# Softmax-attention scores as three products of rounded parts and rests

## The reference, cut to what matters

```
q = apply_rope(q, cos, sin) * (DA_DH ** -0.5)
k = apply_rope(k, cos, sin)
s = jnp.einsum('bhmqd,bhmkd->bhmqk', q_blk, k).astype(jnp.float32)
p = jax.nn.softmax(s, axis=-1)
a = p[:, :, 0] - lam * p[:, :, 1]
```

## Time and profile before

| what | value |
|---|---|
| median of 3 runs | 2431.71 us (2431.59 to 2432.74) |
| the profiled execution | 2431.39 us, span 2429.6 us |
| TensorE matmuls busy | 2413.4 us, 99% of the span |
| VectorE busy | 1827.1 us, 75% |
| ScalarE busy | 1300.5 us, 54% |
| GpSimd busy | 201.6 us, 8% |
| TensorE's share of the chain that ended last | 95% |

### The profile page before, as it was taken

The page is one execution under the profiler, slowest core; times in us unless marked ns, Lnnn a source line. Parts: engine busy times, 40 slices in busy tenths (PEclk is TensorE's granted clock), DMA queues, the critical chain, the costliest instruction groups (busy, mean ns, idle before and its releaser), DMA issues.

```text
span 2429.6 us, 40806 instructions
## 1 busy us (share of the span) xinstructions
PE 2413.4 (99%) x16410; PEld 2250.9 (93%) x16410; DVE 1827.1 (75%) x2403; ACT 1300.5 (54%) x2014; POOL 201.6 (8%) x236
## 2 busy tenths in 40 slices
PE   9999999999999999999999999999999999999998
PEld 9999989898999999888899998999989999998887
DVE  6666777754888998978585567777648889999784
ACT  6444666543555556556454456664436555554563
POOL 0001022100200000003100011111002000000031
PEclk9999999999999999999999999999999999999999
DMA  5454444254323233833233544343543232346421
GB/s 178 139 177 139 137 133 146 102 180 152 105 72 96 87 103 106 302 113 130 97 128 125 180 146 140 127 134 107 192 148 105 72 90 83 107 159 250 149 100 61
DMA packets 290411, 321.52 MB, mean 132 GB/s; under 512 B 10416, under 2 KB 223920, under 8 KB 290224
## 3 DMA queue, kind: packets, MB, share of 16 engines
q1 hardware_dynamic: 215744, 171.39, 22.6%
q10 hardware_dynamic: 74480, 147.53, 16.7%
HBM read 253.60 MB, written 65.27 MB: 131 GB/s over the span
## 4 chain that ended last, share of the span: by engine, by line
PE 95%; ACT 2%; issue 1%; DVE 1%; DMA 1%; POOL 0%; ACTq 0%; SPq 0%; DVEq 0%; POOLq 0%
PE ps L862 23%; PE ps L1142 14%; PE ps L1324 13%; PE ps L1087 9%; PE ps L835 5%; PE ps L1430 5%; PE ps L1070 5%; PE ps L1293 3%; PE ps L1260 3%; PE ps L849 3%; PE ps L1040 2%; PE ps L914 1%; PE ps L1410 1%; PE ps L1059 1%; PE ps L971 1%
## 5 line engine op out<-in xcount | busy, mean ns | idle before, releaser
L2048 DVE TENSOR_TENSOR wlo<-raw,whi 128x1024 fp32r<-128x1024 f32 (+1 forms) x152 | 163.8, 1079 | 55.1 <-ACT whi L3016 55.1
L862 PE MATMUL ps<-hT_hi,whi 128*128 128x384 f32 x608 | 203.1, 334 | 0.0
L862 PE MATMUL ps<-hT_hi,wlo 128*128 128x384 f32 x608 | 203.1, 334 | 0.0
L862 PE MATMUL ps<-hT_lo,whi 128*128 128x384 f32 x608 | 203.1, 334 | 0.0
L3030 ACT ACTIVATE U<-ps 128x384 f32<-128x384 f32 x152 | 74.8, 492 | 223.8 <-PE ps L862 223.8
L1324 PE MATMUL ps<-whi,PH_hi 128*128 128x512 f32 x456 | 179.1, 393 | 0.0
L1324 PE MATMUL ps<-whi,PH_lo 128*128 128x512 f32 x456 | 177.7, 390 | 0.0
L1324 PE MATMUL ps<-wlo,PH_hi 128*128 128x512 f32 x456 | 177.5, 389 | 0.0
L1508 DVE TENSOR_TENSOR wlo<-raw,whi 128x2048 fp32r<-128x2048 f32 x53 | 123.0, 2320 | 68.5 <-ACT whi L2368 68.4
L1636 DVE TENSOR_TENSOR wlo<-raw,whi 128x1024 fp32r<-128x1024 f32 (+1 forms) x98 | 102.8, 1069 | 79.3 <-ACT whi L2536 79.2
L862 PE MATMUL ps<-S_hi,whi 128*128 128x384 f32 x456 | 152.3, 334 | 0.0
(11 more groups left out here) (333 smaller groups left out, 7002.1 us busy)
## 6 DMA issues: line engine op xcount, KB each, us to landing
raw<-w_up_dram SPq DMA_DIRECT2D x88, 512.0 KB
raw<-w_in_dram SPq DMA_DIRECT2D x64, 512.0 KB
raw<-w_down_dram SPq DMA_DIRECT2D x60, 512.0 KB, 4.7
raw<-w_in_dram SPq DMA_DIRECT2D x16, 1024.0 KB
zT<-gst ACTq DMA_DIRECT2D x40, 384.0 KB, 2.4
GT<-zT ACTq DMA_DIRECT2D x16, 768.0 KB, 6.0
pD<-CG ACTq DMA_DIRECT2D x26, 384.0 KB, 2.3
zT<-hn ACTq DMA_DIRECT2D x48, 192.0 KB, 1.8
```

The lines of the kernel that those rows point to most:

```text
L862: ins = mm(ps[:, 4 * (j % 2) + bank, 0:TH], quarter(L, W[y], j, (w,))[:, 0, k * P:(k + 1) * P], sum_operand(a, x, k), start=(opens and k = ...
L2048: v.tensor_tensor(lo, x, hi.bitcast(F32), ALU.subtract)\
```

## The change

After the rotation, QK is split into QK_hi and QK_lo (float32r), each in two parts: "prompt" (columns 0 to 255) and "sample" (256 to 767). The high part is a copy on ScalarE, the low part a subtraction on VectorE. QK_lo lies where QK lies and QK_hi where QKs (the half-swapped copy that the rotation adds) lies. The scores become three rounds of products; a round has one product per map. Core of the diff:

```diff
+SPLIT = {"prompt": (0, TP), "sample": (TP, T)}
+        QK_lo, QK_hi = stack(x_off, h_off, [("QK_lo", [P, 2, T], F32R), ("QK_hi", [P, 2, T], F32R)])
+        A_hi = steps("att_turned_high", ["prompt", "sample"])
+        A_lo = steps("att_turned_low", ["prompt", "sample"])
             def att_scores(it, q):
                 if q == 0:
-                    pe.wait_ge(A_rope.sem, A_rope.at(it, "radd"))
+                    pe.wait_ge(A_lo.sem, A_lo.at(it, "prompt"))
...
-                for m in range(2):
-                    rows_ = slice(m * DA_DH, (m + 1) * DA_DH)
-                    ins = mm(ps[:, AB[m], 0:kn], QK[rows_, 0, q * P:(q + 1) * P], QK[rows_, 1, k0:k0 + kn], start=True, stop=True)
+                if q == TP // P:
+                    pe.wait_ge(A_lo.sem, A_lo.at(it, "sample"))
+                QK_ = (QK_hi, QK_lo)
+                for i, (x, y) in enumerate(PASSES):
+                    for m in range(2):
+                        rows_ = slice(m * DA_DH, (m + 1) * DA_DH)
+                        ins = mm(ps[:, AB[m], 0:kn], QK_[x][rows_, 0, q * P:(q + 1) * P], QK_[y][rows_, 1, k0:k0 + kn],
+                                 start=(i == 0), stop=(i == 2))
```

```diff
             def gla_output(it, following):
...
                 v.tensor_copy(O1[:, 4:NT, :], view(ps[:], GB[1] * 512, [[P, NT - 4], [1, P]])).then_inc(*G_out.step("o"))
+                if following:
+                    att_low(it + 1, "prompt")
                 done(G_sq, it, "sq")
+            def att_low(it, part):
+                c0, c1 = SPLIT[part]
+                done(A_hi, it, part)
+                v.tensor_tensor(QK_lo[:, :, c0:c1], QK[:, :, c0:c1], QK_hi[:, :, c0:c1].bitcast(F32), ALU.subtract).then_inc(*A_lo.step(part))
                     if k + 1 < NT:
                         att_max(it, k + 1)
+                    if h and k == 0:
+                        att_low(it, "sample")
                     in_sum(L, e, "c12")
+                    if not more:
+                        att_low(L * NH, "prompt")
+                        att_low(L * NH, "sample")
```

```diff
+            def att_high(it, part):
+                c0, c1 = SPLIT[part]
+                done(A_rope, it, "radd")
+                a(QK_hi[:, :, c0:c1], QK[:, :, c0:c1], ACT.Copy).then_inc(*A_hi.step(part))
                     act.dma_start(abD[(NH + h) * P:(NH + h + 1) * P, :], ab2).then_inc(ab_st[1], 16)
+                    att_high(it + 1, "prompt")
...
                     att_exponentials(it + 1, 0)
+                    att_high(it + 1, "sample")
...
+                att_high(L * NH, "prompt")
+                att_high(L * NH, "sample")
                 gla_silu(L * NH)
                 gla_sigmoids(L * NH)
```

More of the change, by code:

```diff
@@ L1722, in copy_level, with gla_output @@
                     .then_inc(*G.step(f"cp{l}"))
-            def gla_output(it):
+            def gla_output(it, following):
                 done(G_pe, it, "o")
@@ L1802, in mixers @@
                     att_rope(it + 1, L, "radd")
-                gla_output(it)
+                gla_output(it, following)
                 if following:
```

## The result

| what | before | after |
|---|---|---|
| median | 2431.57 us (6 runs) | 2447.86 us (6 runs, 2445.81 to 2448.96) |
| ratio, 95% interval | | 1.0065 [1.0055, 1.0076] |
| profiled execution | 2431.39 us | 2447.8 us |

The change makes the kernel 16.3 us slower. The forecast was 2443.5 us, range 2437 to 2452.

The account below looks back on a forecast made before the run. TensorE, busy 99% of the span, was taken as the bound. Entry 12.8 plus turns 4.8 minus score savings 5.2 and 0.3 gave +12.1 us on 2431.39, so 2443.5 us, range 2437 to 2452.

Parts of the forecast that it names:

- The entry: Start of each layer: high copies wait on ScalarE before the silu; TensorE 6.4 us later per layer, 12.8 in all.
- The turns: From one head to the next, three per layer: split work delays TensorE 0.94 + 0.5 + 0.94 us, 4.8 us in all.
- The scores: TensorE's score blocks: 0.90 us for 1.06 (512 keys), 0.57 for 0.63 (256); 5.2 and 0.3 us saved.
- The low part of the sample in later heads: VectorE, after the second row maximum of heads 1 to 3: costed at nothing; uncovered, 6.6 us.
- the clock is held: TensorE's clock stays full throughout: 2438 to 2447 us, chance 0.56.
- the fall: Rival: TensorE's clock halves in the entry's new gap, up to 5.8 us more per layer, 2445 to 2455 us; chance 0.22.
- no overlap: Rival, score blocks: rounded products of the two array halves do not run side by side, 2467 us; chance 0.07.

## Why the prediction held, and where it was off

- **The entry.** Forecast 6.4 us per layer, measured 6.1 in both (first layer: table load 233.24 for 232.9, c21's end 240.8 for 240.4, row maximum's end 249.2 for 249.2, last part of level 0 at 254.60 for 254.6). The two runs that put the copies elsewhere confirm that it is the order and not the work.
- **The turns.** Forecast 0.94 + 0.5 + 0.94 us per layer; the jumps were 0.94, 0.52, 0.91 in the first layer and 0.98, 0.63, 0.92 in the second, 4.9 us in all for 4.8.
- **The scores.** 0.89 us for 0.90 and 0.56 us for 0.57. The saving measured alone is 5.4 us for 5.5. By the Trainium skill, page "TensorE: Matmul & The Clock Gate", section "Wait — 56ns, not 53.3ns?", 216 ns for 512 columns, the saving would have been 6.5 us, an estimate (the prediction has 6.6). The measured round is 0.23 us.
- **The sum.** With the clock held the terms measured are 12.3 + 4.9 - 5.4 = 11.8 us, and 2443.35 - 2431.57 is 11.8. That the total came within 0.15 us of the forecast is in part luck: the entry was forecast 0.5 us too dear, the turns and the scores each 0.1 us off, and the executions of that kernel themselves spread from 2442.81 to 2444.04. Some sums of the prediction are slightly off, by nothing that matters: 32 x 0.16 is 5.1, not 5.2; the case without overlap adds up to 2467.8, not 2467; the low end of the range to 2438.1, not 2437.
- **The low part of the sample in later heads** was costed at nothing, and the lateness between tiles 1 and 2 of heads 1 to 3 never grows.
- **The step that failed** is the choice that the clock is held: it stood as likeliest with 0.56, the fall as a rival with 0.22. It fell in both layers and cost 4.5 us of the 16.3. (The prediction says that no stretch of the trace before tests this. Its last microseconds do: the last matmul ends at 2422.5 us and the granted clock is at half from 2427.6.) With the clock kept up by fillers the time is 2443.35 for a forecast of 2443.5. So the changed kernel's 2447.86 lies in the range because its upper end allowed for the clock, not by the sum itself: +12.1 us forecast, +16.3 measured. The rival's price was a bound, up to 5.8 us per layer, for side work at half speed from its first product to its 48th; measured it is 2.2 us per layer in the medians (2.7 and 2.2 in the traces). Half speed began already in the gap, where it costs nothing, and only 6.1 and 4.9 us of it lay behind the last wait.
- **The pairs.** The rival "no overlap" was given 0.07 and argued from the float32 records alone. The rounded ones pair up too, even when they are issued half by half.

What stays open: why in the run with the high copies moved the clock fell in the second layer and not in the first, though the waits are alike (1.0, 0.5 and 1.2 to 1.3 us in both), was not tried. The length of the stretch at half clock also differs from one execution to the next with nothing changed at the entry: 10.2 and then 6.8 us in the changed kernel, 6.8 and then 10.2 with the products map by map, 6.8 twice with the turn's copies moved. No run shows why.

## What to carry to other kernels

In a kernel whose bound engine has almost no waits, price a new instruction by what stands behind it in its engine's order, not by its length: two copies of 1.5 us together cost 6.1 us in each layer, since they waited 6.8 us for an input ahead of work that did not need it. Put a waiting step behind everything that is ready before it, and prefer the place where the input has just come. When a new gap on TensorE is forecast, add the price of the lower clock to its likeliest case (here about half of the time from the end of the last wait to the clock's return), and look whether the gap can be filled or, better, made to go: moving the copies and the low part took away the gap and the clock's loss together.

## What the runs showed of the hardware that was not expected

- TensorE reordered matmuls across the two 64-row halves: three products of one half issued ahead of three of the other still ran in pairs, and the block took 0.90 us, as with alternating products (0.89 us).
- The clock fell within the gap of 3.8 us (at 250.5), and twice about the end of a wait of only 1.2 to 1.3 us that came soon after others (1457.8 in the run with the entry's high copies moved, after waits of 1.0 and 0.5 us; 254.6 with one gap filled); in the kernel with two filled gaps it never fell. Fillers of 3.8 us kept it up in one layer and not in the other.
